# A hybrid attention step on one core: half of each layer's first MLP products in pairs of seven block products

## The reference, cut to what matters

```python
D_MODEL, D_FF = 1024, 4096
def _residual(x, mix, p):
    x = x + _rmsnorm(mix, p['g_post_mix'])
    f = jnp.square(jax.nn.relu(_rmsnorm(x, p['g_pre_mlp']) @ p['w_ff1'])) @ p['w_ff2']
    return x + _rmsnorm(f, p['g_post_mlp'])
```

## Time and profile before

| what | value |
|---|---|
| median of three runs | 2262.19 us |
| profiled execution, its own time | 2264.05 us |
| its span in the profile | 2262.3 us |
| TensorE busy | 2220.9 us (98%) |
| VectorE, ScalarE, GpSimd busy | 918, 1000, 990 us (41, 44, 44%) |
| DMA, mean | 83 GB/s |

### The profile page before, as it was taken

How to read it: one execution, slowest core, us unless ns; L and a number is a source line. 1 busy time by engine, 2 the same in 40 slices (tenths; PEclk the granted TensorE clock), 3 DMA queues, 4 the chain that set the end, 5 groups by cost and what they waited for, 6 DMA issues and landing times.

```text
span 2262.3 us, 40494 instructions
## 1 busy us (share of the span) xinstructions
PE 2220.9 (98%) x16914; PEld 2127.2 (94%) x16914; DVE 917.8 (41%) x2019; ACT 999.9 (44%) x1915; POOL 989.5 (44%) x782
## 2 busy tenths in 40 slices
PE   7999999999999999999999999999999999999997
PEld 7999988899999999999999999888999999999997
DVE  5677555535415300001576775455253261001014
ACT  4554433434655642332344554444255565332412
POOL 3423324445564464544423332244456636544532
PEclk9999999999999999999999999999999999999999
DMA  5122321122224122222321223111212321222221
GB/s 192 64 74 73 94 72 57 57 74 66 66 85 172 48 90 88 85 84 66 122 91 54 83 82 92 56 57 57 83 57 75 139 99 66 89 89 85 85 91 63
DMA packets 59381, 187.84 MB, mean 83 GB/s; under 512 B 8224, under 2 KB 17248, under 8 KB 58560
## 3 DMA queue, kind: packets, MB, share of 16 engines
q1 hardware_dynamic: 50976, 169.28, 22.8%
q10 hardware_dynamic: 8224, 15.97, 1.9%
HBM read 170.99 MB, written 10.89 MB: 80 GB/s over the span
## 4 chain that ended last, share of the span: by engine, by line
PE 91%; DVE 5%; ACT 2%; issue 1%; DMA 1%; POOL 0%; SPq 0%; DVEq 0%; ACTq 0%
PE dense L943 44%; PE att L943 31%; PE att L1250 1%; PE att L1160 1%; PE att L1180 1%; PE att L1017 1%; PE dense L972 1%; DVE h_raw L1937 1%; PE att L1208 1%; PE att L1099 1%; PE att L1095 1%; PE att L1325 1%; PE att L1081 1%; PE att L1292 1%; PE att L1184 1%
## 5 line engine op out<-in xcount | busy, mean ns | idle before, releaser
L2335 POOL TENSOR_TENSOR wlo<-wraw,whi 128x1024 fp32r<-128x1024 f32 x245 | 589.0, 2412 | 545.5 <-ACT whi L1377 545.5
L943 PE MATMUL dense<-h_hi,whi 128*128 128x280 f32 x1888 | 557.3, 295 | 2.6 <-DVE qr L1837 1.5
L943 PE MATMUL dense<-h_lo,whi 128*128 128x280 f32 x1888 | 550.4, 292 | 0.0
L943 PE MATMUL dense<-h_hi,wlo 128*128 128x280 f32 x1888 | 549.3, 291 | 0.0
L1377 ACT ACTIVATE whi<-wraw 128x1024 fp32r<-128x1024 f32 x302 | 315.2, 1051 | 266.9 <-DMA wraw<-in_w 265.8
L943 PEld LDWEIGHTS dense<-h_hi,whi 128*128 128x128 f32 x1888 | 355.0, 188 | 14.2 <-issue 9.1
L943 PEld LDWEIGHTS dense<-h_hi,wlo 128*128 128x128 f32 x1888 | 354.5, 188 | 0.7
L943 PEld LDWEIGHTS dense<-h_lo,whi 128*128 128x128 f32 x1888 | 354.8, 188 | 0.0
L943 PE MATMUL att<-h_hi,whi 128*128 128x280 f32 x1024 | 299.2, 292 | 0.4 <-issue 0.4
L943 PE MATMUL att<-h_lo,whi 128*128 128x280 f32 x1024 | 298.4, 291 | 0.0
L943 PE MATMUL att<-h_hi,wlo 128*128 128x280 f32 x1024 | 297.8, 291 | 0.0
(11 more groups left out here) (393 smaller groups left out, 4582.6 us busy)
## 6 DMA issues: line engine op xcount, KB each, us to landing
wraw<-in_w SPq DMA_DIRECT2D x302, 512.0 KB, 3.5
x_spill<-x ACTq DMA_DIRECT2D x2, 2240.0 KB, 7.7
x<-x_spill ACTq DMA_DIRECT2D x2, 2240.0 KB, 12.3
k_cat<-k_rope SPq DMA_DIRECT2D x16, 212.0 KB, 3.5
x<-in_x SPq DMA_DIRECT2D x4, 560.0 KB, 6.5
out_y_out<-x SPq DMA_DIRECT2D x4, 560.0 KB, 3.1
out_c_out<-ckv SPq DMA_DIRECT2D x2, 560.0 KB, 5.5
const<-in_const SPq DMA_DIRECT2D x1, 1112.0 KB, 12.9
```

The costliest lines, as they stand in the source:

```text
L943: mm = pe.matmul(bank(u, o, hf)[0:m, :], a[:, k, o * 128:o * 128 + m], b[:, k, H[hf]], start=(k == 0 and i == 0), stop=(k == kt - 1 and i ...
L2335: pool.tensor_tensor(wlo[slot][:, :], wraw[slot][:, :], whi[slot][:, :].bitcast(F32), ALU.subtract).then_inc(pool_done, st.done("pool", f" ...
```

## The change

In each layer the first products of hidden tiles 16 to 31 are computed in eight pairs. For a pair, the weights of two output tiles and the eight input blocks form a 2 x 2 block matrix (even and odd tile x first and last four input blocks), and the input another (first and last four blocks x first and second token half). Their product takes seven block products in place of eight: four of the seven use sums or differences of weights, four use sums or differences of tokens.

- One block product is 4 blocks x 3 matmuls of 280 columns, so a pair is 84 matmuls.
- VectorE forms the four token differences once per layer: ten subtractions and additions of 128 x 1120, and four more for their low parts (`token_sums`); ScalarE makes the four high parts.
- For each pair VectorE forms four sums of weights of 128 x 512 (`weight_sums`); the last is written over the odd unit's first half. ScalarE makes three more high parts of 128 x 512, GpSimd three more low parts.
- A pair's products add up in three PSUM banks with the start flag off, and VectorE takes copies between them (`strassen`, "kept"). The relu is then taken from SBUF by ScalarE on 560 columns.
- The second products of groups 1 and 2 are taken by half groups of four hidden tiles ("ff2 two": one unit holds two output tiles x four blocks, loaded by two DMAs), so that pairs and second products alternate: four ff2 units, pair 0, then two units and a pair by turns, up to pair 6; pair 7 follows pair 6 directly, and then come the eight second products of group 3.
- A sixth weight slot (`SUMS`) is added in this stage.

The core of the diff:

```diff
+def run_order():
+
+    two = {g: [KIDX["ff2 two", 4 * g + d] for d in range(4)] for g in HALF_GROUPS}
+    pair = [KIDX["ff1 sums", n] for n in STRASSEN]
+    order = list(range(UIDX["ff2", 7] + 1))
+    order += two[2] + pair[0:1]
+    for i, g in enumerate((3, 4, 5)):
+        order += two[g][0:2] + pair[2 * i + 1:2 * i + 2] + two[g][2:4] + pair[2 * i + 2:2 * i + 3]
+    order += pair[7:8]
+    return order + [UIDX["ff2", n] for n in range(24, 32)]
...
+                def strassen(u):
+                    n = KINDS[u][1]
+                    for v in (u - 2, u - 1, u):
+                        pe.wait_ge(act_done, A("act", f"w hi {v}"))
+                        pe.wait_ge(pool_done, A("pool", f"w lo {v}"))
...
+                    def product(w, x, at_, first, name):
+                        for k in range(4):
+                            for i, (a, b) in enumerate(((0, 0), (1, 0), (0, 1))):
+                                mm = pe.matmul(bank(u, *at_), w[a][:, k, :], x[b][:, k, :], start=(first and k == 0 and i == 0),
+                                               stop=(k == 3 and i == 2), skip_group_check=True)
+                        mm.then_inc(pe_done, st.done("pe", name))
+
+                    def token_sum(i):
+                        if n == STRASSEN[0]:
+                            pe.wait_ge(act_done, A("act", f"t hi {i}"))
+                            pe.wait_ge(dve_done, A("dve", f"t lo {i}"))
+
+                    wait_bank(u, *low)
+                    product(a11, b11, low, True, f"product 1 {u}")
+                    wait_bank(u, *top)
+                    product(a12, b21, top, True, f"product 2 {u}")
+                    wait_bank(u, *mid)
+                    token_sum(0)
+                    product(s1, t1, mid, True, f"product 5 {u}")
+                    token_sum(1)
+                    pe.wait_ge(dve_done, A("dve", f"kept 1 {u}"))
+                    product(s2, t2, low, False, f"product 6 {u}")
+                    pe.wait_ge(dve_done, A("dve", f"kept 5 {u}"))
+                    product(s4, b22, mid, False, f"half {u} 0 1")
+                    token_sum(2)
+                    pe.wait_ge(dve_done, A("dve", f"kept 6 {u}"))
+                    product(s3, t3, low, False, f"product 7 {u}")
+                    token_sum(3)
+                    product(a22, t4, top, True, f"half {u} 1 0")
...
+                def strassen(u):
+                    for i, parts in enumerate(((f"early early {u}", f"evac {u} 0 1"), (f"late late {u}", f"evac {u} 1 0"))):
+                        n = KINDS[u][1] + i
+                        for part in parts:
+                            act.wait_ge(dve_done, A("dve", part))
+                        t = hid1[0][:, n % 8, :]
+                        link(act.activation(t, t, ACT.Relu))
+                        act.activation(t, t, ACT.Square).then_inc(act_done, st.done("act", f"hid {n}"))
+                        round_tile(hid1[2][:, n % 8, :], t, (act_done, A("act", f"hid {n}")), f"hid hi {n}")
...
+                def weight_sums(u):
+                    n = KINDS[u][1]
+                    even, odd = (wraw[slot_of[l, v]] for v in (u - 2, u - 1))
+                    for v in (u - 2, u - 1):
+                        dve.wait_ge(w_loaded[slot_of[l, v]], loads[l, v])
+                    if n > STRASSEN[0]:
+                        dve.wait_ge(pe_done, A("pe", f"half {KIDX['ff1 sums', n - 2]} 0 1"))
+                    a11, a12, a21, a22 = (t[:, first:first + 512] for t in (even, odd) for first in (0, 512))
+                    link(dve.tensor_tensor(s_raw[0][:, :], a21, a22, ALU.add), f"sum 0 {u}")
+                    link(dve.tensor_tensor(s_raw[1][:, :], s_raw[0][:, :], a11, ALU.subtract), f"sum 1 {u}")
+                    dve.tensor_tensor(sums[2][0], by_k(a12), sums[1][0], ALU.subtract).then_inc(dve_done, st.done("dve", f"sum 2 {u}"))
+                    dve.tensor_tensor(a21, a11, a21, ALU.subtract).then_inc(dve_done, st.done("dve", f"s3 {u}"))
...
+                    if i == 0:
+                        dve.wait_ge(pe_done, A("pe", f"dense {UIDX['ff2', KD - 1]}"))
+                        for j, a, b in ((0, (0, 1), (0, 0)), (2, (1, 1), (0, 1))):
+                            link(dve.tensor_tensor(raw[j], part(h_hi, *a), part(h_hi, *b), ALU.subtract))
+                            link(dve.tensor_tensor(raw[j], raw[j], part(h_lo, *a), ALU.add))
+                            link(dve.tensor_tensor(raw[j], raw[j], part(h_lo, *b), ALU.subtract), f"t raw {j}")
+                    if i == 1:
+                        for j, a, t in ((1, (1, 1), 0), (3, (1, 0), 1)):
+                            link(dve.tensor_tensor(raw[j], part(h_hi, *a), raw[t], ALU.subtract))
+                            link(dve.tensor_tensor(raw[j], raw[j], part(h_lo, *a), ALU.add), f"t raw {j}")
+                    if i == 2:
+                        low(0)
+                        low(2)
+                    if i == 3:
+                        low(1)
+                        low(3)
...
+                    dve.wait_ge(pe_done, A("pe", f"dense {KIDX['ff2 two', 4 * (n // 4 - 2) + 3]}"))
+                    dve.wait_ge(pe_done, A("pe", f"product 1 {u}"))
+                    link(dve.tensor_copy(even[:, H[0]], low), f"kept 1 {u}")
+                    dve.wait_ge(pe_done, A("pe", f"product 2 {u}"))
+                    dve.tensor_tensor(even[:, H[0]], even[:, H[0]], top, ALU.add).then_inc(dve_done, st.done("dve", f"early early {u}"))
+                    keep(5, mid)
+                    keep(6, low)
+                    add_kept(6, mid, even[:, H[1]], f"half {u} 0 1", f"evac {u} 0 1")
+                    if n == ADJOINED[0]:
+                        weight_sums(KIDX["ff1 sums", ADJOINED[1]])
+                    add_kept(5, low, odd[:, H[1]], f"product 7 {u}", f"late late {u}")
+                    link(dve.tensor_copy(odd[:, H[0]], low), f"evac {u} 0 0")
+                    dve.wait_ge(pe_done, A("pe", f"half {u} 1 0"))
+                    dve.tensor_tensor(odd[:, H[0]], odd[:, H[0]], top, ALU.add).then_inc(dve_done, st.done("dve", f"evac {u} 1 0"))
...
+                    kind, n = KINDS[u]
+                    if kind.startswith("ff1 "):
+                        pool.wait_ge(dve_done, A("dve", f"sum 2 {KIDX['ff1 sums', n]}"))
+                    if kind == "ff1 sums":
+                        for i, (raw, lo, hi) in enumerate(sums):
+                            pool.wait_ge(act_done, A("act", f"w hi {u} {i}"))
+                            pool.tensor_tensor(lo, raw, hi.bitcast(F32), ALU.subtract).then_inc(pool_done, st.done("pool", f"w lo {u}" if i == 2 else None))
+                        return
+                    if kind == "ff1 even":
+                        pool.wait_ge(dve_done, A("dve", f"s3 {u + 2}"))
                     slot = slot_of[l, u]
                     pool.wait_ge(act_done, A("act", f"w hi {u}"))
...
                         w_lo(step[1])
+                    elif step[0] == "strassen":
+                        for n in range(KINDS[step[1]][1], KINDS[step[1]][1] + 2):
```

In the planner, the split of a pair's weights (its sums, then the even and the odd unit) is placed only after the pair before it is done, with one exception, for the last pair:

```diff
+                if step == ("strassen", KIDX["ff1 sums", ADJOINED[0]]):
+                    for v in (0, -2, -1):
+                        key = split.pop(0)
+                        assert key == (l_, KIDX["ff1 sums", ADJOINED[1]] + v), key
+                        assert v == 0 or done_at[slot_before[key]] + 2 <= now, key
+                        full.append((l_, ("w", key[1])))
```

More of the change, by code:

```diff
@@ L86 @@
 UIDX = {u: n for n, u in enumerate(UNITS)}
+STRASSEN = range(2 * KD, 4 * KD, 2)
+ADJOINED = STRASSEN[-2:]
+HALF_GROUPS = range(2, 6)
+KINDS = UNITS + [(kind, n) for n in STRASSEN for kind in ("ff1 even", "ff1 odd", "ff1 sums")] + [
+    ("ff2 two", 4 * g + d) for g in HALF_GROUPS for d in range(4)]
+KIDX = {u: n for n, u in enumerate(KINDS)}
+def run_order():
[7 more added lines that the diff above has]
+    return order + [UIDX["ff2", n] for n in range(24, 32)]
+RUN = run_order()
 def outs_of(kind):
-    return (2, 4) if kind in ("up_a", "up_b") else (1, KD)
+    return (2, 4) if kind in ("up_a", "up_b", "ff2 two") else (1, KD)
 CONST = {}
@@ L414, in source @@
                     return "hid%d" % (n // 8 % 2)
+                if kind == "ff2 two":
+                    return "hid1"
                 return "h"
@@ L421, in ready_names @@
                     return ("act", "ob hi 4"), ("pool", "ob lo 4")
+                if kind == "ff2 two":
+                    unit = 4 * (n // 4) + k
+                    return ("act", f"hid hi {unit}"), ("pool", f"hid lo {unit}")
                 if s.startswith("hid"):
@@ L612, in layer_plan @@
                         plan.append((l, ("split_y", n)))
+                    if (kind, n) == ("ff2", 7) or (kind == "ff2 two" and n in range(8, 11)):
+                        plan.append((l, ("token sums", 0 if kind == "ff2" else n - 7)))
                     if u == U_MIX[-1]:
@@ L645, in program @@
             for l_, u, o, hf in halves:
```

(24 more changed lines are left out.)

192 lines of the change are left out of this document (145 added, 47 removed).

## The result

The changed kernel takes 2297.76 us (median; 2295.12 to 2298.82), the kernel before 2262.53 (2261.93 to 2263.56) on the same chip: ratio 1.0154, 95% interval 1.0136 to 1.0171. The forecast was 2299, range 2272 to 2313. The profiled execution took 2298.82 with a span of 2297.1, so 34.8 us more than the span of the one before (2262.3), 17.4 per layer; the forecast was 18.5.

The account below looks back on a forecast made before the run. TensorE, busy 98% of the span, was taken as the bound. Per layer 8.5 + 9.6 + 9.1 + 2.0 + 1.6 - 12.3 = +18.5 us, +37 for two: 2301 profiled, 2299 as median; range 2272 to 2313.

Parts of the forecast that it names:

- Gain of 12.3: Eight pairs save 96 matmuls a layer at 0.1282 us each: 12.3 us.
- Pair 0, 8.5: Ahead of pair 0 TensorE waits for free banks and GpSimd's low parts: 0.3 + 0.9 + 3.4 + 3.9 = 8.5 us.
- The turns: VectorE instructions with two SBUF inputs and GpSimd's exclude each other, an instruction each, in every token and weight sum.
- The clock at pair 0, taken as nothing: At pair 0 the forecast counted no clock loss, the gaps of 3.4 and 3.9 us having work between them.
- more clock lost: Rival: clock also falls at pair 0, token sums slower, pair 7 costs the full 2.7 us; 2312 us, chance 0.14.
- Pairs 1 to 6, 1.6 each: Before each of these pairs TensorE waits 1.6 us for GpSimd's low parts, 9.6 us a layer.
- Pair 7, 9.1 and clock 2.0: Before pair 7 TensorE waits 9.1 us for GpSimd's five low parts; the clock falls, costing 2.0 more.
- Group 3's second products, 1.6: Right after pair 7 these need its hidden tiles and wait 1.6 us for the odd tile's low part.
- At nothing: Two DMAs per unit, kept copies, ScalarE's high parts and the guarded loads were taken to cost nothing.
- no turns: Rival: collisions of VectorE and GpSimd at SBUF cost little; +4.4 us a layer, 2271 us, chance 0.13.
- faster: Rival: GpSimd's parts are there when TensorE arrives, only the last 1.6 us lost; -10.7 a layer, 2241 us, chance 0.04.

Follow-up runs that it names:

- e12: e10 with the last two low parts of the token sums made within pair 0, each just ahead of the product that takes it; 2251.89 us.
- e4: The changed kernel with the low parts of both weight tiles made on VectorE instead of GpSimd for pairs 1 to 7; 2276.43 us.
- e6: The changed kernel with one input of each of the four weight sums read from PSUM, so values differ; 2290.58 us.
- e5: The changed kernel with 60 matmuls whose product nobody reads placed between pair 6 and pair 7; 2294.45 us.
- e3: The changed kernel with the last pair (tiles 30 and 31) replaced by two ordinary units behind pair 6; 2279.57 us.
- e1: The changed kernel with every pair replaced by its two ordinary units, leaving the half groups alone; 2265.03 us.
- e7: The changed kernel with products reordered, each awaiting its own operands, evictions following, and pair 7's sums started in two steps within pair 6; 2259.07 us, 2259.43 on another chip.
- e10: e7 with the four low parts of the token sums spread one, one and two behind units before pair 0, instead of two and two; 2266.04 us.
- e8: e7 with one unit of second products moved from between pairs 4 and 5 to before pair 0; 2265.18 us.
- e9: e7 with two units of second products moved to before pair 0, leaving one unit before pair 4 and before pair 5; 2279.98 us.

## Why the prediction held, step by step

The number came out within 1.3 us and the chains are the ones forecast, but that it came out so closely is in part luck: one term was too high and a loss put at nothing made up for it. Per layer in us, forecast and what layer 0 shows:

- *Gain of 12.3*: 96 fewer matmuls a layer; products run 12 in 1.54, 0.128 each, the strided weights too. Right. The best version (e12) keeps 11.2 us of the 24.6 that two layers save.
- *Pair 0, 8.5*: from VectorE's last eviction (start 882.78) to pair 0 (914.18) lie 31.4 us with 192 matmuls, 24.7, in them: 6.7 lost. The parts that the waits name: 2.7 for banks, about 3.4 for GpSimd (19.2 of L1051's waits less 8.6 and six of 1.2). I had 4.6 and 3.9. The turns are there (GpSimd's split at 905.77 took 2.36 for 1.25, the two behind it 5.74 for 4.8), but the longest wait for a bank was 2.3 and not 3.4. Size too high by 1.8.
- *The clock at pair 0, taken as nothing*: 2.9 lost in layer 0, 1.6 in layer 1 (12 matmuls in 3.10). That part of the rival "more clock lost" was true, at less than its 4.0. In layer 0 of e4 the slow stretch fell a few us earlier and delayed nothing; in layer 1 it cost 1.8. This is the step I left out; it hid the error in the one before.
- *Pairs 1 to 6, 1.6 each*: period 24.6 where 180 matmuls are 23.1: 1.5 each, 1.2 of it idle and 0.24 because 12 matmuls after such a stop took 1.78 in place of 1.54: the first one counts with its whole length there (0.37 us at pair 6) and not with the step of 0.13. The chain is as forecast: the first sum stretched to 1.13, the third done, then GpSimd's five parts. e4 removes the wait by taking two of the five away, e6 part of it by taking the turns away.
- *Pair 7, 9.1 and clock 2.0*: idle 8.6, and 1.8 for its slow matmuls (1.6 of it clock by e5); 2.6 in layer 1, where they took 13.41 us. e3 gives 9.1 per layer back with 1.5 of extra matmuls, so 10.6 for both: right.
- *Group 3's second products, 1.6*: 1.6, as forecast.
- *At nothing*: the half groups, DMAs and evictions: 2 us in all by e1, of which 0.8 per layer is a wait for a hidden tile.

Sum of the rows for layer 0: 6.7 + 2.9 + 9.0 + 8.6 + 1.8 + 1.6 - 12.3 = 18.3. With layer 1's two clock terms in place, 1.6 and 2.6, the same sum is 17.8. The traces bear both out. In layer 0 the first norm's matmuls at the end of the MLP moved from 1114.14 to 1132.22 while the MLP's start moved by -0.3, so the stage grew by 18.4. In layer 1 the start of the MLP's first products moved by 17.0 (one stands at 1878.66 before and 1895.66 after) and the last norm's matmuls by 34.8 (2250.43 and 2285.24), so it grew by 17.8. The spans' mean of 17.4 is lower because 1.1 us come back between the MLPs, in layer 1's attention, which the change leaves as it was, and 0.3 before the first. Of the rivals, "no turns" fell by e6 and by the stretched sums (the prediction counts four rows for turns in rows 9; there are three of VectorE); "faster" fell as argued, in this order of products. But its condition, GpSimd's parts there when TensorE comes, was nearer than I wrote ("only GpSimd at twice its shown speed"): e7 met it at pairs 1 to 6 entirely, with the same work in another order.

## What to carry over

Fewer products pay only once their operands' preparation is out of the way: follow the last operand through the slower engines, and let each product wait for its own, the latest-made one last, before giving up on the arithmetic. An engine that both evicts and prepares should have each preparation placed where TensorE has some products in hand (e12), not two in a row (e7, e10). A unit moved to cover one gap opens another wherever it stood, and the next one may read what was just made (e8, e9).
